# Every second matmul of a weight stream walks its moving operand and its output columns from the last to the first

## The reference

```
proj = h @ w_in[l]                      # 2048 x 7184
x = x + mixed @ w_out[l]
q = (h @ w_q) ; k, v = split(mem_n @ w_kv) ; ... @ w_o
u = causal_dwconv(h @ w_up, conv_w) + conv_b ; (silu(gate) * up) @ w_down
p = h @ fox_w_in[j] ; x = x + y @ w_out
p = h @ swa_w_in[j] ; x = x + y @ w_out
```

## Time and profile before

| | |
|---|---|
| median of 3 runs | 2169.59 us (2169.34 to 2169.61) |
| profiled execution, first to last instruction (span) | 2167.6 us |
| its own time, beside the span | not recorded by itself; the runs lie 2.0 us above the span |
| mean granted TensorE clock | 0.999 of full speed |
| TensorE matmul, busy | 2156.3 us, 99% |
| TensorE weight load (beside matmuls) | 1865.8 us, 86% |
| VectorE, ScalarE busy | 75%, 61% |
| DMA queue with the weights, share of 16 engines | 50.2% |

### The profile page before, as it was taken

One profiled execution on the slowest core, in us unless ns is written; L12 is line 12 of the kernel. 1 busy time (PEld: TensorE's weight loads), 2 busy tenths in 40 slices (PEclk: granted clock), 3 DMA queues, 4 the chain that ended last, 5 costly groups with the idle time before them and its releaser, 6 DMA issues.

```text
span 2167.6 us, 34503 instructions
## 1 busy us (share of the span) xinstructions
PE 2156.3 (99%) x13406; PEld 1865.8 (86%) x13406; DVE 1618.3 (75%) x2945; ACT 1327.2 (61%) x2601; POOL 9.7 (0%) x22
## 2 busy tenths in 40 slices
PE   9999999999999999999999999999999999999998
PEld 8888888888888888888888888888888888888887
DVE  7898666786688877655778867777676767688774
ACT  7866447775576666544666656555556655567764
POOL 0000000000000000000000000000000000000000
PEclk9999999999999999999999999999999999999999
DMA  7443434665455555555555555545554455544453
GB/s 279 169 146 137 147 115 141 218 217 186 156 190 189 188 191 186 193 185 192 187 191 189 185 194 185 193 171 197 181 177 174 167 192 186 189 161 155 146 200 140
DMA packets 107619, 389.31 MB, mean 180 GB/s; under 512 B 12304, under 2 KB 12560, under 8 KB 106688
## 3 DMA queue, kind: packets, MB, share of 16 engines
q1 hardware_dynamic: 105264, 377.31, 50.2%
q0 software_dynamic: 1904, 9.47, 1.2%
q10 hardware_dynamic: 288, 0.32, 0.0%
HBM read 384.34 MB, written 2.13 MB: 178 GB/s over the span
## 4 chain that ended last, share of the span: by engine, by line
PE 95%; DVE 3%; ACT 1%; issue 0%; DMA 0%; SPq 0%; DVEq 0%; ACTq 0%
PE main L510 88%; PE two L510 6%; PE two L513 1%; DVE WL L987 1%; DVE gt L987 0%; DMA RAW<-ws 0%; DVE GQ L993 0%; ACT L1654 0%; ACT WH L1655 0%; DVE GK L993 0%; PE main L556 0%; ACT PP L1655 0%; DVE PB L987 0%; ACT NT L1655 0%; DVE PP L993 0%
## 5 line engine op out<-in xcount | busy, mean ns | idle before, releaser
L1655 ACT ACTIVATE WH<-RAW 128x512 fp32r<-128x512 f32 x1416 | 882.1, 629 | 657.6 <-PE main L510 651.1
L987 DVE TENSOR_TENSOR WL<-RAW,WH 128x512 fp32r<-128x512 f32 x1416 | 961.2, 687 | 383.9 <-ACT WH L1655 374.4
L510 PE MATMUL main<-A,WH 128*128 128x512 f32 (+1 forms) x3680 | 1141.9, 393 | 1.0 <-DVE WL L987 1.0
L510 PEld LDWEIGHTS main<-A,WL 128*128 128x128 f32 x3584 | 673.9, 188 | 154.8
L510 PE MATMUL main<-A,WL 128*128 128x256 f32 x3584 | 713.7, 278 | 0.0
L510 PEld LDWEIGHTS main<-A,WH 128*128 128x128 f32 x3680 | 562.7, 189 | 13.8 <-issue 9.3
L510 PE MATMUL main<-H,WH 128*128 128x512 f32 x704 | 221.1, 395 | 0.0
L510 PE MATMUL main<-B,WH 128*128 128x512 f32 (+1 forms) x640 | 184.4, 373 | 0.0
L510 PEld LDWEIGHTS main<-H,WL 128*128 128x128 f32 x704 | 132.3, 188 | 31.3
L510 PE MATMUL main<-H,WL 128*128 128x256 f32 x704 | 138.4, 278 | 0.0
L510 PE MATMUL main<-WH,A 128*128 128x512 f32 (+1 forms) x448 | 137.6, 380 | 0.0
(11 more groups left out here) (322 smaller groups left out, 1722.5 us busy)
## 6 DMA issues: line engine op xcount, KB each, us to landing
RAW<-ws SPq DMA_DIRECT2D x707, 512.0 KB, 3.3
CB<-cscr POOLq DMA_DIRECT2D x4, 1024.0 KB, 4.7
XT<-xT POOLq DMA_DIRECT2D x4, 512.0 KB, 6.0
MS<-memT POOLq DMA_DIRECT2D x4, 512.0 KB, 8.7
xs<-xT SPq DMA_DIRECT2D x7, 256.0 KB, 7.6
out<-YT SPq DMA_DIRECT2D x7, 256.0 KB, 2.6
CST<-cst SPq DMA_DIRECT2D x1, 1248.0 KB, 7.9
G<-g POOLq DMA_DIRECT2D x1, 1024.0 KB, 5.9
```

The lines of the kernel that those rows point to most:

```text
L510: return e.matmul(o, l, r, start=start, stop=True, skip_group_check=True)
L987: return e.tensor_tensor(o, a, b, op)
L1655: return e.activation(o, i, f, bias=bias, scale=scale, accum_out=accum)
```

## The change

A helper `back` is added: a matmul whose output columns and whose moving columns both go from the last to the first. Column c of the output still belongs to column c of the moving operand; the sums are the same. In the wide form the matmuls into the second bank go through it; in the tokens, plain and small forms the second of three. The order, the operands, the number of instructions, the waits and the stationary operands stay. The branches for the ends of `w23` and `xv` stay as they were.

```diff
             def mm(o, l, r, start=True):
                 return e.matmul(o, l, r, start=start, stop=True, skip_group_check=True)
 
+            def back(o, l, r, start=True):
+                return mm(o[:, ::-1], l, r[:, ::-1], start)
+
...
                         cols = [slice(256 * r + 128 * t, 256 * r + 128 * t + 128) for t in range(2)]
-                        for t in range(2):
-                            mm(P[:, t, :], h[:, cols[t]], both, start=first and r == 0)
-                        for t in range(2):
-                            ins = mm(P[:, t, 0:T], l[:, cols[t]], hi, start=False)
+                        mm(P[:, 0, :], h[:, cols[0]], both, start=first and r == 0)
+                        back(P[:, 1, :], h[:, cols[1]], both, start=first and r == 0)
+                        mm(P[:, 0, 0:T], l[:, cols[0]], hi, start=False)
+                        ins = back(P[:, 1, 0:T], l[:, cols[1]], hi, start=False)
...
                             mm(P[:, t, 0:n], hi, h[:, cols], start=first and r == 0)
-                            mm(P[:, t, 0:n], hi, l[:, cols], start=False)
+                            back(P[:, t, 0:n], hi, l[:, cols], start=False)
                             ins = mm(P[:, t, 0:n], lo, h[:, cols], start=False)
...
                         mm(o, h[:, cols], X[:, kt, 0, :], start=first and (r == 0 if form == "small" else r % 2 == 0))
-                        mm(o, l[:, cols], X[:, kt, 0, :], start=False)
+                        back(o, l[:, cols], X[:, kt, 0, :], start=False)
                         ins = mm(o, h[:, cols], X[:, kt, 1, :], start=False)
```

## The result

The changed kernel takes 2193.4 us (2193.07 to 2193.64, 4 runs) against 2169.6 us (2169.34 to 2170.1) for the kernel before: ratio 1.0108, 95% interval 1.0093 to 1.0122. It is slower by 23.8 us, 4.5 ns for each of the 5296 turned matmuls.

What follows compares the result with a forecast made beforehand. The prediction took TensorE's stream of matmuls, busy 99% of the span, as the bound. Gap below, gap above and columns were each taken as nothing, sum 0 us, so 2169.6 us, range 2072 to 2240 us, held at 81%.

Steps and rivals of the forecast that it cites:

- the forecast itself, no effect: Whole kernel: turned matmuls change neither gap nor column rate, sum 0 us, time 2169.6 us (2165.3 to 2173.9); chance 36%.
- rival 3: Turned matmuls: each starts late, slower by up to a gap each, 70 us, giving 2240 us; chance 19%.
- The bound: Whole kernel: TensorE's matmuls are busy 99% of the span, so changes in stream matmul intervals go straight into the time.
- The law, columns plus a fixed gap: All stream forms: each matmul pays one cycle per column plus a fixed gap of some 13.5 ns.
- A cost that takes no notice of a jump should take none of a jump saved: Stream matmuls: the gap ignores where an operand starts, so turning the walk saves nothing; taken as 0 us.
- The plain triple: Plain form: its third matmul continues the second's read, its output starts over, yet its interval is 120 ns like the others.
- the 231 ns at the start of w20: Three triples at w20's start take 231 ns a matmul; the prediction left room for the gap to move by 4 ns.
- The columns: Turned matmuls: a descending column takes the same one cycle as an ascending one, so no cost.
- rival 2: Turned matmuls: downward columns run at half rate, two cycles each, 855 us slower, 3025 us; chance 19%.
- the meeting in a PSUM word: Tokens and plain forms: a downward walk starts at the PSUM word just written and must await its sum; rival 3's reason.
- The other sign that I named: Timeline interval behind a turned 512-column matmul: 233 ns if unchanged, 220 or less by rival 1, 246 by rival 3.
- Rival 1: Stream matmuls: reads starting where the last ended save gaps, up to 97 us, 2072 us (half: 2121); chance 26%.

## Why the prediction was right or wrong

The time lies in the range (2072 to 2240) and on the side that was given 38%, but the forecast itself, no effect, was wrong. That the range holds the time is no merit of the mechanism, since it reached over both signs. What came was rival 3 by sign and size, at a third of the price that stood as its bound (23.8 of 70 us).

- **The bound: right.** The stream's intervals went straight into the time: 24.7 us by intervals, 24.2 by spans. VectorE and ScalarE stayed at 1621.1 and 1326.5 us (1618.3 and 1327.2 before).
- **The law, columns plus a fixed gap: half right.** 57 ns over 640 in a pass stand, but the gap isn't fixed. It moved between 688 - 640 = 48 ns a pass (upwards, the first pass of a half at an offset of 240 bytes) and 716 - 640 = 76 (changed directions, at 96 bytes) with nothing but the weights' place and the direction changed. Nor was it the same before: the wide gap of 13.6 ns came from a window's count, while the chain has 696.8 ns a pass, 14.2 ns each, against 13.3. The tight 227 and 120 ns of the kernel before are what one layout gives.
- **"A cost that takes no notice of a jump should take none of a jump saved": the step that failed.** The plain triple that it rests on the earlier trace rows is a single layout and a single form; it showed that a continued walk isn't cheaper, not that the gap is deaf to addresses. The sign to the contrary was in my hand, the 231 ns at the start of w20, and the wide form's own intervals (233, 233, 115, 118), which a law of a fixed gap would have at 227, 227, 120, 120. I let them stand as room of some ns. Room of 4.5 ns on each turned matmul is the whole result. The runs showed in its place that the gap follows both how the moving operand is read (2193.19 us with the read turned alone) and where the weights lie (2189.12 us with them 96 bytes further).
- **The columns: right.** A downward column takes one cycle like an upward one; rival 2 (19%, 3025 us) is out by 830 us. On the rule from Advanced Engine Details and Errata of the Trainium skill, section Memory Cachelines, that a non-contiguous pattern slows matmuls significantly: in PSUM a step of -1 is not such a pattern, turning the write alone gives a ratio of 1.0000. In SBUF it costs 10 ns of 697, far from a second cycle for each of the 768 turned columns, 320 ns.
- **Rival 3: right in sign, not in its reasons.** Of its two reasons, the meeting in a PSUM word is refuted by the run with only the write turned. A late start of each downward read fits neither form: in the wide one two turned matmuls cost 10 ns and one of them alone 16, and in the tokens form one costs 5 to 15, two cost 17 to 20 and all three 17. The test that I named for it, that only the triple would grow, came out the other way: the pass grew by 10 ns, the triple by 4.5. The other sign that I named, the interval behind a turned 512-column matmul (233, 220 or 246 ns), looked in the wrong place: it stands at 234, and the growth is behind the two with lo weights.
- **Rival 1: not seen in the wide form.** With the buffers where they lie only the plain form gained, 7 ns a triple, 1 us in all, and it gains 8 from a move of the weights by 96 bytes as well, so that no turn is needed for it. At other offsets the tokens form gains up to 6 ns a triple and the plain one loses, which isn't the saving of a start at the place where the last read ended, as that place is the same at every offset.
- **A sum and a reading were wrong.** 721 ns a pass would be 555 matmuls in 100 us, not 545; the 568 that came lie between 576 and 555. The fp32 matmuls of the earlier trace rows start 215.7 ns apart by the finer starts of the trace, not 213; that their gap is small, 2.4 ns, stays true.

## What to carry to other kernels

Where TensorE streams without a wait, as here, the interval between fp32r matmuls has some ns above its columns (7 to 23 on average in these runs, from the plain triples of 341 ns in two buffers of the kernel with 64 bytes of padding to the tokens triples of 709), and it depends on how the moving operand is walked and on where the two operands lie modulo 256 bytes, and not on these alone. A gap that is the same in all rows of one layout is not thereby a constant. In the wide form keep the moving operand's walk upwards; in the others time it, as the sign changes with the place. When a buffer is moved or padded, move it by multiples of 256 bytes unless the new place has been timed: 256 bytes cost nothing here and 96 cost 19 us. Such prices don't add over neighbours, so time the whole pattern, which one kernel that changes the pattern from chunk to chunk does for all sixteen at once.

## What the runs showed of the hardware that I had not expected

- Writing PSUM from the last column to the first is free (2169.99 against 2170.12 us), reading SBUF so isn't (2193.19).
- The interval depends on the weights' place, and a move by 256 bytes is no move: it gives a ratio of 1.0000, one by 96 gives 1.0088.
- The same turned matmul costs 9 ns a tokens triple at one place of the weights and saves 6 at another.
- With l1 alone turned, the wide passes alternate between 705 and 695 ns, in an order that isn't tied to addresses.
- A weight load of 32 columns takes 109 ns against 189 for 128 and doesn't shorten the pass (694 against 697 ns), nor the price of the direction (9 against 10 ns). What in the read makes that price stays open.
